# Transformer-like decoder trunk on one core: the embedding's gate weights read once per layer, the dense expert loop ending at chunk 54 instead of 58

## What is computed

```python
def hybrid_layer(x, ...):
    ...                                             # three token mixers, gates
    x = x + (g_a * y_a + g_b * y_b + g_c * y_c) @ w_out
    hf = rms_norm(x, norm_ffn).reshape(b * seq, d)
    x = x + peer_ffn(hf, ...).reshape(b, seq, d)
    x = x + jax.nn.sigmoid(rms_norm(x, ple_norm) @ ple_w_gate) * (pe @ ple_w)
    return x

def peer_ffn(...):                                  # per token and head (8 heads)
    # top 16 of 128 x 128 experts by product keys, softmax over the 16 scores
    act = gelu(einsum('td,thkd->thk', xt, expert_u[idx]))
    return einsum('thk,thkd->td', gate * act, expert_v[idx])
```

## Time and profile before

| | before |
|---|---|
| median of 3 runs | 4369.83 us (4365.32 to 4370.94) |
| profiled execution: own time | 4365.77 us |
| its span, first to last instruction | 4364.0 us |
| TensorE busy, share of the span | 3831.0 us, 88% |
| VectorE / GpSimd / ScalarE busy | 2714.0 / 1636.7 / 912.6 us |
| moved by DMA | 1063.83 MB, mean 244 GB/s |
| mean granted TensorE clock | 0.936 of full |

### The profile page before, as it was taken

One profiled execution on the slowest core, in us unless ns is written; L12 is line 12 of the kernel. 1 busy time (PEld: TensorE's weight loads), 2 busy tenths in 40 slices (PEclk: granted clock), 3 DMA queues, 4 the chain that ended last, 5 costly groups with the idle time before them and its releaser, 6 DMA issues. The chain is left out here.

```text
span 4364.0 us, 43792 instructions
## 1 busy us (share of the span) xinstructions
PE 3831.0 (88%) x15856; PEld 2832.5 (65%) x15856; DVE 2714.0 (62%) x5304; ACT 912.6 (21%) x1953; POOL 1636.7 (38%) x1552
## 2 busy tenths in 40 slices
PE   8789999967999999994797899999679999999937
PEld 7546787856766666652684467888567666666516
DVE  4865216658567666777658651165685676667775
ACT  2243302236200000000122532021461000000001
POOL 6612000023355555566375120000243554555563
PEclk9789999988999999997897899999899999999968
DMA  2001233348899999999620012333579999999996
GB/s 100 29 29 39 74 135 124 121 173 294 323 390 401 403 392 410 375 410 403 250 80 29 30 39 84 135 123 125 193 278 340 391 400 403 394 409 376 410 383 253
DMA packets 300550, 1063.83 MB, mean 244 GB/s; under 512 B 41648, under 2 KB 75056, under 8 KB 274992
## 3 DMA queue, kind: packets, MB, share of 16 engines
q0 software_dynamic: 147456, 536.94, 32.0%
q1 hardware_dynamic: 119312, 488.44, 29.5%
q10 hardware_dynamic: 33568, 35.65, 2.3%
HBM read 1025.27 MB, written 35.65 MB: 243 GB/s over the span
## 5 line engine op out<-in xcount | busy, mean ns | idle before, releaser
L2040 POOL DMA_INDIRECT u_rows<-in_peer_u,idx_all x512 | 663.9, 1297 | 1652.3 <-DVEq L1943 933.2
L1647 PE MATMUL bank<-v_tile,shared 128*128 128x512 f32 x2048 | 906.1, 597 | 14.2 <-DVE shared L1990 13.9
L1963 DVE SCALAR_TENSOR_TENSOR x<-v_rows,act_w,x 128x1024 f32<-128x1024 f32 x512 | 657.6, 1284 | 206.1 <-DMA v_rows<-in_peer_v,idx_all 176.1
L2040 POOL DMA_INDIRECT v_rows<-in_peer_v,idx_all x512 | 587.7, 1148 | 453.9 <-DVE x L1963 337.8
L1647 PEld LDWEIGHTS bank<-v_tile,shared 128*128 128x128 f32 x2048 | 391.8, 192 | 467.2 <-issue 444.6
L1951 DVE CUSTOM_DVE_ANT_0 u_rows<-u_rows,h 128x1024 f32<-128x1024 f32 x512 | 605.8, 1223 | 99.1 <-DMA u_rows<-in_peer_u,idx_all 98.2
L1635 PE MATMUL bank<-hT,bT 128*128 128x256 f32 x2048 | 452.5, 379 | 0.0
L1635 PEld LDWEIGHTS bank<-hT,bT 128*128 128x128 f32 x2048 | 388.4, 190 | 72.0 <-issue 22.0
L1538 PE MATMUL bank<-hT,ring 128*128 128x256 f32 x1536 | 341.0, 383 | 14.4 <-PEq L150 14.4
L1538 PEld LDWEIGHTS bank<-hT,ring 128*128 128x128 f32 x1536 | 293.6, 192 | 56.7 <-issue 16.0
L1817 ACT ACTIVATE shared<-bank 128x512 f32<-128x512 f32 x128 | 76.2, 595 | 1023.4 <-PE bank L1647 948.7
(11 more groups left out here) (362 smaller groups left out, 5311.2 us busy)
## 6 DMA issues: line engine op xcount, KB each, us to landing
v_tile<-in_peer_v SPq DMA_DIRECT2D x256, 512.0 KB, 7.2
ring<-in_w_in_panels SPq DMA_DIRECT2D x76, 1024.0 KB, 4.8
bT<-in_peer_ut SPq DMA_DIRECT2D x128, 512.0 KB, 7.3
ring<-in_peer_w_query SPq DMA_DIRECT2D x32, 1024.0 KB, 4.8
aT<-in_peer_ut SPq DMA_DIRECT2D x64, 512.0 KB, 6.7
sT<-in_peer_ut SPq DMA_DIRECT2D x64, 512.0 KB, 7.2
gates<-dense_gates SPq DMA_DIRECT2D x32, 1024.0 KB, 10.7
ring<-in_ple_w_gate SPq DMA_DIRECT2D x24, 1024.0 KB, 7.6
```

What stands on the lines that cost most here:

```text
L1647: ins = mm(acc[t][part][:, :], act_pair[p % AHEAD][:, at:at + P], v_tile[:, e % DENSE, part * 512:part * 512 + 512], start=(e == 0), stop= ...
L1963: stt(out=m.x[:, 2 + t, :], in0=vr[:, n % RINGS, :], scalar=act_w[:, p % 4, i:i + 1], in1=m.x[:, 2 + t, :], op0=ALU.mult, op1=ALU.add).the ...
L2040: nc.gpsimd.indirect_dma_start(out=rows[:, n % RINGS, :], out_offset=None, in_=table, in_offset=bass.IndirectOffsetOnAxis(ap=idx_all[:, t, ...
```

## The change

DENSE_END goes from 58 to 54, so that the dense pairs and the `add` lie four chunks earlier in the list, and the items of the embedding are laid out anew: tiles 0 and 1 take one panel beside each of chunks 56 to 59, and tile 2 takes its norm behind chunk 60, its transposes behind 61 and two panels beside each of 62 and 63. The gate weights of the embedding are read once per layer: three panels stay in the three slots of the ring, the fourth goes to the upper half of `hT` (no longer needed once all `pre` products are done), and all three units use them.

```diff
--- before.py
+++ after.py
@@ -1338,7 +1338,7 @@
 OCT_PAIRS = OCT // 2
 QUADS = HALF_T // 4
 HOT_CHUNKS = 8
-DENSE_END = 58
+DENSE_END = 54
 
 
 def tail_order():
@@ -1403,14 +1403,14 @@
             order += [("add",), ("embed", 0)]
         if c == DENSE_END + 1:
             order.append(("turn", 0))
-        for unit in range(2):
-            at = DENSE_END + 2 + 3 * unit
-            if at <= c < at + 2:
-                order += [("embedded", unit, n) for n in (2 * (c - at), 2 * (c - at) + 1)]
-        if c == DENSE_END + 3:
+        if DENSE_END + 2 <= c < DENSE_END + 6:
+            order.append(("embedded", 0, c - DENSE_END - 2))
+        if c == DENSE_END + 6:
             order.append(("embed", 1))
-        if c == DENSE_END + 4:
+        if c == DENSE_END + 7:
             order.append(("turn", 1))
+        if DENSE_END + 8 <= c < DENSE_END + 10:
+            order += [("embedded", 1, n) for n in (2 * (c - DENSE_END - 8), 2 * (c - DENSE_END - 8) + 1)]
     order += [("embed", 2), ("turn", 2)] + [("embedded", 2, n) for n in range(4)]
     return order
 
@@ -1429,7 +1429,7 @@
     nc, io = m.nc, m.io
     with ExitStack() as ctx:
         s = semaphores(m, COMMON + " wg_in keys_in gain_in p_in comb_ready rms_ready h_ready topped exp_done selected u_free v_free "
-                       "dsel_ready gelu_done out_free ple_rms ple_h ple_added slots_turned slots_here left_ready left_scaled right_ready hot_filled hot_read "
+                       "dsel_ready gelu_done out_free ple_in ple_rms ple_h ple_added slots_turned slots_here left_ready left_scaled right_ready hot_filled hot_read "
                        "stored0 stored1 pre_in0 pre_in1 pre_in2 pre_in3 v_in0 v_in1 v_in2 v_in3 gate_in0 gate_in1 "
                        "pre_done pre_read gated v_done dense_added")
         sb = lambda n, shape, dt=F32: ctx.enter_context(nc.sbuf_tensor(f"{n}_{layer}", shape, dt))
@@ -1480,6 +1480,7 @@
         pre_w = [a.rearrange("p k n -> p (k n)").rearrange("p (k c) -> p k c", k=KD)
                  for a in (m.aT[:, :, :], m.sT[:, :, :], m.bT[:, 0:2, :], m.bT[:, 2:4, :])]
         dsel = v_tile[:, :, :].rearrange("p a d -> p (a d)")[:, 0:6 * P].rearrange("p (a t n) -> p a t n", a=3, t=2)
+        last_panel = m.hT[:, 4:8, :].rearrange("p k n -> p (k n)")
         staging = [a[:, :, :].rearrange("p a d -> p (a d)").rearrange("p (e t) -> p e t", t=STORE_T) for a in (v_tile, gates)]
         dram = io.gates[layer]
         pre_in = s.pre_in0, s.pre_in1, s.pre_in2, s.pre_in3
@@ -1501,7 +1502,7 @@
                 sources.append((io.w_out[layer, what[2]], KD, PANEL))
             if what[0] == "query":
                 sources.append((io.peer_w_query[layer, what[2]], KD, PANEL))
-            if what[0] == "embedded":
+            if what[0] == "embedded" and what[1] == 0 and what[2] < RING:
                 sources.append((io.ple_w_gate[layer, what[2]], KD, PANEL))
         panels = Panels(m, s, sources, early=RING)
         gate_count, out_count, turned_count, query_count, score_count, ple_count, sig_count = ({} for _ in range(7))
@@ -1527,6 +1528,7 @@
             to_vec = Banks(pe, m.banks[2:4], s.vec_filled, s.vec_read)
             mm = nc.tensor.matmul
             loaded = iter(range(len(sources)))
+            kept = []
 
             def panel():
                 return panel_view(panels.landed(pe, next(loaded)), KD)
@@ -1666,13 +1668,18 @@
                     pe.wait_ge(s.p_in, 16 * 4)
                     pe.wait_ge(s.act_read, ple_count[unit][0])
                     pe.wait_ge(s.vec_read, ple_count[unit][1])
-                w = panel()
+                if n == RING:
+                    pe.wait_ge(s.ple_in, 16)
+                    w = panel_view(last_panel, KD)
+                else:
+                    if unit == 0:
+                        kept.append(panel())
+                    w = kept[n]
                 bank = to_act.open()
                 for t in unit_at(unit):
                     for k in range(KD):
                         ins = mm(bank[:, cols(t)], ple_hT[:, k, t * P:(t + 1) * P], w[:, k, :], start=(k == 0), stop=(k == KD - 1))
                 ins.then_inc(s.act_filled, 1)
-                panels.released.append((s.act_filled, to_act.n))
                 bank = to_vec.open()
                 for t, tile in zip(unit_at(unit), UNITS[unit]):
                     for k in range(2):
@@ -1722,12 +1729,17 @@
                 sp.wait_ge(s.hot_filled, QUADS)
                 sp.dma_start(gain[:, :], io.ple_norm[bass.ds(layer, 1), :].partition_broadcast(P).rearrange("p l d -> p (l d)")).then_inc(s.p_in, 16)
                 sp.wait_ge(s.pre_done, KEYS)
+                sp.dma_start(last_panel, io.ple_w_gate[layer, RING].rearrange("p k c -> p (k c)")).then_inc(s.ple_in, 16)
                 sp.dma_start(pT, weight(io.p, layer, 0, 2, 0, T)).then_inc(s.p_in, 16)
                 for k in range(2):
                     sp.dma_start(w_ple[k], io.ple_w[layer, k * P:(k + 1) * P, :]).then_inc(s.p_in, 16)
 
+            def embedded(unit, n):
+                if unit == 0 and n < RING:
+                    panel()
+
             loads = iter(range(len(sources)))
-            parts = {"gate": panel, "mix": panel, "out": panel, "query": panel, "embedded": panel, "pre": pre, "values": values, "add": add}
+            parts = {"gate": panel, "mix": panel, "out": panel, "query": panel, "embedded": embedded, "pre": pre, "values": values, "add": add}
             for what, *n in order:
                 if what in parts:
                     parts[what](*n)
```

## The result

| | before | changed |
|---|---|---|
| median | 4369.65 us (4365.32 to 4370.94, 4 runs) | 4422.81 us (4418.02 to 4428.24, 4 runs) |
| ratio | | 1.0121, 95% interval 1.0109 to 1.0133 |
| profiled execution: own time, span | 4365.77, 4364.0 us | 4425.17, 4423.3 us |
| moved by DMA | 1063.83 MB | 1047.05 MB |

The change costs 53 us; 34 were forecast (4404 us against 4369.83). It moves 16.8 MB less and takes 1.2% longer.

The account below looks back on a forecast made before the run. It took TensorE to bound the dense loop, DMA bytes (b) and VectorE's program order (c). Per layer -10.7 + 28.3 = +17.6 us, +35.2 for two, gave 4404 us, slower by 0.8%; range 4378 to 4430.

Parts of the forecast that it names:

- R3: Rival: gathered rows come late in (c), 1 us more in nine chunks, +18 us, 4422 us; chance 0.12.
- (b): End of the dense part, 4096 to 4235.8 us, paced by DMA bytes; forecast -10.7 us per layer, to about 129.
- (c): Embedding beside the last chunks, add to last gathered row, limited by VectorE's program order; +28.3 us per layer, about 120.
- Dense loop (a): The dense loop, to about 4096 us, bound by TensorE's matmuls back to back; forecast change 0.
- Three chunks more before VectorE at the end of the loop: At 4096 us VectorE has chunks 46 to 63 ahead instead of 49 to 63: one fewer in (b), four more in (c).
- fuller rings: Row rings starting (b) fuller thanks to slack in the dense loop: -3 us per layer, net of the last head's selection.
- with those gone I drop it: In (c), the 2.44 us wait for the last v row, dropped because the panel loads beside it are removed.
- Eight panel loads removed: 8.4 MB fewer loads, all in (c), where DMAs had room and VectorE's own time hid them: 0 beyond the other terms.
- (d): Tile 3's own embedding after the last gathered row, 36.2 us; the same chain follows, so forecast change 0.
- Its signs: Profile signs: (b) 120 to 137 us, (c) 118 to 124, embedding-product waits about 3 per layer, row waits under 3.
- R4: Rival: TensorE cold in (c), panels at 1.2 GHz taking 17.3 us each, +35 us, 4439 us; chance 0.05.
- R1: Rival: bytes decide over (b) and (c) together, -10.6 us per layer, 4349 us, faster; chance 0.07 with anything like it.

Follow-up runs that it names:

- e1_end54: The kernel before with DENSE_END = 54 and nothing else, all twelve panels loaded and the old order kept: 4453.75 us, ratio 1.0189.
- e11_select_early2: The changed kernel with the last two heads' selection two chunks earlier, and their queries and scores early enough for it: 4425.14 us, ratio 1.0122.
- e3_reread: The changed kernel, but with all twelve gate panels loaded per layer as before: 4434.05 us, ratio 1.0146.
- e2_kept58: The changed kernel with DENSE_END = 58 and the order of before, gate weights still kept on chip: 4374.8 us, ratio 1.0010.
- e10_half_rows: The changed kernel with gathered rows of 512 columns instead of 1024 from chunk 56 on, same number of issues: 4418.39 us, ratio 1.0106.

## Why the prediction was right, and where it was off

The forecast was slower by 34 us; it was 53, within the range. The measured 4422.81 us is R3's 4422 almost to the us, and that is luck: R3 added 9 us of late rows per layer to a forecast that had (b) 5 us too short, and (c) brought 4 of its 9 while (b) brought the other 5. By its own steps:

- **Dense loop (a): 0.** Right. From the first `pre` matmul to the start of (b) it took 965.7 us before and 965.8 after in layer 1, 967.0 and 968.7 in layer 0. That TensorE "was never idle" holds only for the later part: of the 966 us of layer 1 it was busy 916, before and after, and early on it waited 49 us for ScalarE, the same in both.
- **Three chunks more before VectorE at the end of the loop.** Right. In (b) and (c) of layer 1 GpSimd made 74 + 39 = 113 issues before and 68 + 71 = 139 after; 24 more were counted, 26 came.
- **(b): -10.7, came out -5.6.** The bytes were right, -3.15 MB by count and 56.8 to 54.0 MB by the windows. The term of -3 for fuller rings was wrong: no head start showed, and e1_end54, without the fourth panel, gained 8.6 us for 4.19 MB where bytes alone would give 10.3. The missing 2 us are the lower rate, 400 GB/s instead of 406. e11_select_early2 shows that the selection was no part of it, and e3_reread the fourth panel's own cost, 2.7 us. The 358 GB/s that the Trainium skill gives as the HBM limit of a core for traffic from HBM to SBUF (DMA: Bandwidth & Descriptors, Where 436 GB/s comes from) was no limit here: every (b), on this one core, moved 395 to 410 GB/s.
- **(c): +28.3, came out +32.3.** The four chunks and the two removed waits were right, and VectorE's sum nearly: 118.0 us measured with no wait for rows, 120 worked out. What failed is "with those gone I drop it" for the waits for rows, 5.8 us above the 118; the sum 2 us too high hid part of it. I took rows that kept up before as rows that would keep up, but before, GpSimd had 25 us of waiting in a stretch of 92, and the change used it up. I had named this as R3 with a chance of 0.12 and 9 us per layer; it came at 5 to 6. R3's "about as much" as 10.3 us for the issues of a chunk was also too low: the earlier trace rows give 47.05 us for 39 issues, 9.7 us for eight, but with the 0.30 us before each that is 12.1, more than the 11.5 that I set against it.
- **Eight panel loads removed: 0.** Right at 58 (e2_kept58), and 5.0 us per layer at 54 net of the fourth panel, already in the sum above, since (c) as forecast had no panels in it.
- **(d): 0.** Right in layer 1, 36.2 and 36.3 us.
- **Its signs.** (b) with 134 us and (c) with 123.8 lie in their ranges. VectorE waited 0.8 and 1.2 us for embedding products, not 3. Row waits in (c) were 5.6 and 4.7 us, not under 3: that one failed.
- **R4, a cold TensorE.** Did not come. VectorE waited 0.8 us for panels. TensorE ran the four one right behind the other, the first in 9.02 us for its 32 matmuls and the next three in 7.07, and it stood idle between such stretches; the mean clock of (c) was 0.73.
- **R1.** Refuted by e2_kept58 and by e10_half_rows: removed loads shortened (c) by 2.1 us and halved rows by 0.6, where R1 would have had some 20 for the first.

Per layer the error is 9.1 us: 5.1 in (b), 4.0 in (c). The mechanism was right, and its two small terms, a credit for rings and a dropped wait, were both taken on the cheerful side.

## What to carry to other kernels

Ask of each stretch which resource ends it, and move work from the one that is full to the one that is not: here work of VectorE and GpSimd was moved out of a stretch held by bytes into one held by VectorE, and lost 32 us to gain 6, while 3 MB moved the same way gained 7 for nothing. Loads that are removed are worth what their stretch waits for them, which here was nothing net at one place of the dense end and 5 us at another. And when a change adds rows to a stretch, look at the idle time of every engine that feeds it, the issuing one too, and not only at the waits that showed before; and count the time between its issues, which its busy time leaves out.

## What was not expected of the hardware

An indirect DMA of 128 rows costs GpSimd as much to issue for 2 KB rows as for 4 KB rows: 93.17 us for 72 issues with half-width rows against 90.89 for 71 (the windows of (c) above), 1.28 to 1.29 us each, with 0.30 us between two. A chunk's eight issues come to 12.7 us by that, more than the 10.14 us that the chunk takes VectorE. In (b) of the changed kernel the mean was 82.96 / 68 = 1.22 us. Single issues range from 0.94 to 1.99 us.

The long issues go with VectorE's work. The 138 issues of the changed kernel from 4128 to 4380 us are sorted here by what VectorE did in the first 0.94 us of each, as the two timelines show it. The 23 that had no kind of VectorE instruction beside them for more than 0.4 us took 0.94 to 1.20 us. The 44 beside the dot products (line 1963) took 1.58 us in the mean, 29 of them over 1.3; the 56 beside the `v` additions (line 1975) 1.16, 12 of them over 1.3. From 3500 to 3900 us it is the same: 40 beside nothing of such length, none over 1.17 us, and 40 beside dot products, mean 1.68. VectorE's dot products and the long issues come together, then; that the one causes the other is not shown, as no run took the dot products away.
